# One 512-column product for h's high and low parts, and the two-step evacuation it needs

## The reference

```
h    = rms_norm(x, norm_pre_w)                     # 256 x 1024
proj = h @ w_in                                    # 1024 x 10256: q,k,v,z of mixer A; beta, decay;
                                                   # q,k,v,z of mixer B; 2 x 1024 gate logits
oa   = gated_delta_rule(silu(conv4(qkv_a)), ...)   # 8 heads of 128, chunked
ob   = moba_attention(qkv_b, T5 bias)              # 8 heads; 256 keys, so causal softmax attention
ya   = rms_norm(oa) * silu(z_a);  yb = ob * silu(z_b)
m    = sigmoid(gate_a) * (ya @ w_branch[0]) + sigmoid(gate_b) * (yb @ w_branch[1])
out  = x + rms_norm(m @ w_out, norm_post_w)
```

## Time and profile before

| | us |
|---|---|
| median of 3 runs (372.27 to 372.52) | 372.43 |
| the profiled execution, its own time | 373.05 |
| its span, from first to last instruction | 371.3 |
| PE busy (share of the span) | 360.4 (97%) |
| DVE busy | 270.6 (73%) |
| ACT busy | 220.4 (59%) |
| POOL busy | 62.3 (17%) |

### The profile page before, as it was taken

The page is one execution under the profiler, slowest core; times in us unless marked ns, Lnnn a source line. Parts: engine busy times, 40 slices in busy tenths (PEclk is TensorE's granted clock), DMA queues, the critical chain, the costliest instruction groups (busy, mean ns, idle before and its releaser), DMA issues.

```text
span 371.3 us, 7660 instructions
## 1 busy us (share of the span) xinstructions
PE 360.4 (97%) x2757; PEld 344.9 (93%) x2757; DVE 270.6 (73%) x558; ACT 220.4 (59%) x500; POOL 62.3 (17%) x121
## 2 busy tenths in 40 slices
PE   8999989999999999999999999999999999999993
PEld 5889977899999999999999999999999999999882
DVE  2868886289957778878788678797786557667644
ACT  5777695344455666767757577666676643534531
POOL 3434844520050000202020201002010100000001
PEclk9999999999999999999999999999999999999998
DMA  8658935958698445554556445564446565874633
GB/s 260 178 172 248 321 117 131 286 129 219 162 234 217 127 121 151 151 148 114 140 131 184 117 114 129 146 181 116 113 124 192 140 195 146 220 221 181 229 113 113
DMA packets 99343, 62.45 MB, mean 168 GB/s; under 512 B 3652, under 2 KB 94190, under 8 KB 99310
## 3 DMA queue, kind: packets, MB, share of 16 engines
q1 hardware_dynamic: 98014, 58.59, 57.3%
q0 software_dynamic: 1296, 3.43, 3.1%
HBM read 60.41 MB, written 1.59 MB: 167 GB/s over the span
## 4 chain that ended last, share of the span: by engine, by line
PE 85%; ACT 4%; DVE 4%; DMA 3%; issue 2%; SPq 1%; DVEq 0%; POOL 0%; ACTq 0%; POOLq 0%
PE banks L1251 61%; PE banks L1465 6%; PE banks L1268 4%; DMA raw<-in_w_in_dram 2%; ACT th_E L674 1%; DVE w_lo L861 1%; PE banks L1350 1%; PE banks L1357 1%; ACT w_hi L634 1%; DVE acc L933 1%; ACT h_hi L647 1%; PE banks L1368 1%; DMA y<-in_dn_onorm_w_dram 1%; PE banks L1393 1%; PE banks L1195 1%
## 5 line engine op out<-in xcount | busy, mean ns | idle before, releaser
L1251 PE MATMUL banks<-h_hi,w_hi 128*128 128x256 f32 x576 | 165.6, 287 | 0.3 <-PE banks L1268 0.3
L1251 PE MATMUL banks<-h_lo,w_hi 128*128 128x256 f32 x576 | 165.4, 287 | 0.0
L1251 PE MATMUL banks<-h_hi,w_lo 128*128 128x256 f32 x576 | 165.0, 287 | 0.0
L861 DVE TENSOR_TENSOR w_lo<-raw,w_hi 128x1024 fp32r<-128x1024 f32 x102 | 124.2, 1220 | 33.1 <-ACT w_hi L634 30.2
L634 ACT CAST w_hi<-raw 128x1024 fp32r<-128x1024 f32 x104 | 107.7, 1046 | 9.3 <-PE banks L1465 4.5
L1251 PEld LDWEIGHTS banks<-h_hi,w_hi 128*128 128x128 f32 x576 | 109.9, 191 | 1.5 <-issue 1.3
L1251 PEld LDWEIGHTS banks<-h_hi,w_lo 128*128 128x128 f32 x576 | 110.0, 191 | 0.0
L1251 PEld LDWEIGHTS banks<-h_lo,w_hi 128*128 128x128 f32 x576 | 109.9, 191 | 0.0
L933 DVE SCALAR_TENSOR_TENSOR acc<-banks,vec,acc 128x255 f32<-128x255 f32 (+2 forms) x72 | 34.5, 479 | 6.2 <-ACT acc L730 3.9
L1251 PE MATMUL banks<-y_hi,w_hi 128*128 128x256 f32 x128 | 36.2, 283 | 0.0
L1251 PE MATMUL banks<-y_lo,w_hi 128*128 128x256 f32 x128 | 36.2, 283 | 0.0
(11 more groups left out here) (235 smaller groups left out, 551.0 us busy)
## 6 DMA issues: line engine op xcount, KB each, us to landing
raw<-in_w_in_dram SPq DMA_DIRECT2D x80, 512.0 KB, 5.2
raw<-in_w_branch_dram SPq DMA_DIRECT2D x16, 512.0 KB, 4.9
raw<-in_w_out_dram SPq DMA_DIRECT2D x8, 512.0 KB, 3.7
xin<-in_x_dram SPq DMA_DIRECT2D x2, 512.0 KB, 3.9
xin<-bias_rows POOLq DMA_DIRECT2D x1, 1024.0 KB, 7.6
th_E<-g_rows POOLq DMA_DIRECT2D x2, 512.0 KB, 5.7
raw<-in_x_dram SPq DMA_DIRECT2D x2, 512.0 KB, 4.8
out_dram<-xin SPq DMA_DIRECT2D x4, 256.0 KB, 2.0
```

The costliest lines, as they stand in the source:

```text
L861: v.tensor_tensor(w_lo[:, t % SLOTS, cols], raw[:, t % SLOTS, cols], w_hi[:, t % SLOTS, cols].bitcast(F32), ALU.subtract).then_inc(s_lo, 1)
L1251: last = mm(ps, w, r, start=i == 0, stop=i == 23)
```

## The change

In 52 tiles (t = 2 to 5 of each head, the last 4 gate tiles, the 16 branch tiles) the two products that share the stationary block `w_hi[k]` become one of 512 columns, since the high and low parts of h (and of y) now lie side by side. The high-part sums stand in the left half of the bank, the low-part ones in the right half, and have to be added when the bank is read. A tile is 8 products of 512 columns and 8 of 256, in parts of 5, 5 and 6. ScalarE copies the right half to SBUF, VectorE adds the left half. For z the `tanh` moves one slot later and reads the sum, and the SiLU two slots later; a bank is free once the sum is made. The other 28 gate and head tiles (gates 0 to 11, t = 0 and 1 of the heads) and the 8 of k_a stay as they are.

```diff
-        h_hi = sb("h_hi", [P, KT, SEQ], F32R)
-        h_lo = sb("h_lo", [P, KT, SEQ], F32R)
+        h_parts = sb("h_parts", [P, KT, 2, SEQ], F32R)
-        y_hi = sb("y_hi", [P, 2, HEADS, SEQ], F32R)
-        y_lo = sb("y_lo", [P, 2, HEADS, SEQ], F32R)
+        y_parts = sb("y_parts", [P, 2, HEADS, 2, SEQ], F32R)
...
# ScalarE, front(h, s): tiles t = 2, 3 and t = 4, 5
-                    nc.scalar.copy(bT[:, t - 2, :], ps).then_inc(s_bT, 1)
-                else:
+                    nc.scalar.copy(bT[:, t - 2, :], bank[n % 2][:, SEQ:]).then_inc(s_b_lo, 1)
+                elif t >= 4 and s % 3 == 0:
+                    sa.wait_ge(s_tile, n + 1)
...
+                    nc.scalar.copy(gza[:, h % 2, :] if t == 4 else gzb[:], bank[n % 2][:, SEQ:]).then_inc(s_z_lo, 1)
+                elif t >= 4 and s % 3 == 1:
                     if h:
                         sa.wait_ge(s_gz, 2 * (h - 1) + t - 3)
-                    ac(tz[:, t - 4, :], ps, ACT.Tanh, scale=0.5).then_inc(s_tz, 1)
+                    sa.wait_ge(s_z_sum, 2 * h + t - 3)
+                    ac(tz[:, t - 4, :], gza[:, h % 2, :] if t == 4 else gzb[:], ACT.Tanh, scale=0.5).then_inc(s_tz, 1)
...
# ScalarE, last 4 gates: gate_front(g, 0) copies the right half, gate_front(g, 1) in the next slot,
# ahead of the w_hi there, waits for s_gate_sum and takes tanh of the sum
-                if part == 0 and n > GATES_B:
-                    gate_front(n - 1 - GATES_B + EARLY)
+                if part < 2 and n > GATES_B:
+                    gate_front(n - 1 - GATES_B + EARLY, part)
...
# ScalarE, branch loop, after split_hi
+                    sa.wait_ge(s_tile, BRANCH0 + i * 4 + t + 1)
+                    if t % 2 == 0:
+                        sa.wait_ge(s_m32, i * 2 + t // 2 + 1)
+                    nc.scalar.copy(m2[:, t % 2, :], bank[t % 2][:, SEQ:]).then_inc(s_m_part, 1)
...
# VectorE, front(h, s)
-                elif s == 9:
+                elif 2 <= t < 4 and s % 3 == 0:
+                    ve.wait_ge(s_b_lo, 2 * h + t - 1)
+                    v.tensor_tensor(bT[:, t - 2, :], ps[:, 0:SEQ], bT[:, t - 2, :], ALU.add).then_inc(s_bT, 1)
+                if s == 9:
...
                 elif t >= 4 and s % 3 == 0:
+                    ve.wait_ge(s_z_lo, 2 * h + t - 3)
+                    gz = gza[:, h % 2, :] if t == 4 else gzb[:]
+                    v.tensor_tensor(gz, ps[:, 0:SEQ], gz, ALU.add).then_inc(s_z_sum, 1)
+                elif t >= 4 and s % 3 == 2:
                     ve.wait_ge(s_tz, 2 * h + t - 3)
-                    v.scalar_tensor_tensor(out=(gza[:, h % 2, :] if t == 4 else gzb[:]), in0=tz[:, t - 4, :], scalar=1.0,
-                                           in1=ps[:, 0:SEQ], op0=ALU.add, op1=ALU.mult).then_inc(s_gz, 1)
+                    ve.wait_ge(s_z_sum, 2 * h + t - 3)
+                    gz = gza[:, h % 2, :] if t == 4 else gzb[:]
+                    v.scalar_tensor_tensor(out=gz, in0=tz[:, t - 4, :], scalar=1.0, in1=gz, op0=ALU.add,
+                                           op1=ALU.mult).then_inc(s_gz, 1)
...
# VectorE, branch loop
                     ve.wait_ge(s_tile, BRANCH0 + i * 4 + t + 1)
-                    if t % 2 == 0:
-                        ve.wait_ge(s_m_hi, d + 1)
+                    ve.wait_ge(s_m_part, i * 4 + t + 1)
+                    v.tensor_tensor(m2[:, t % 2, :], bank[t % 2][:, 0:SEQ], m2[:, t % 2, :], ALU.add).then_inc(s_m_sum, 1)
+                    ve.wait_ge(s_m_sum, i * 4 + t + 3)
...
                     v.scalar_tensor_tensor(out=one(m2[:, t % 2, :]), in0=(th_a if t % 2 else th_b)[:, bass.ds(d, 1), :],
-                                           scalar=1.0, in1=one(bank[t % 2][:, 0:SEQ]), op0=ALU.add,
+                                           scalar=1.0, in1=one(m2[:, t % 2, :]), op0=ALU.add,
                                            op1=ALU.mult).then_inc(s_m2, 1)
...
# TensorE
+            def wide_third(n, t, part, right):
...
+                for i in ((0, 1, 2, 3, 4), (5, 6, 7, 8, 9), (10, 11, 12, 13, 14, 15))[part]:
+                    k = i // 2
+                    if i % 2 == 0:
+                        mm(ps, w_hi[:, slot, P * k:P * k + P], right[:, k], start=k == 0, stop=k == KT - 1)
+                    else:
+                        last = mm(ps[:, 0:SEQ], w_lo[:, slot, P * k:P * k + P], right[:, k, 0], start=False, stop=k == KT - 1,
+                                  skip_group_check=True)
...
-                            pe.wait_ge(s_gz, 2 * (h - 1) + t + 1)
+                            pe.wait_ge(s_z_sum, 2 * (h - 1) + t + 1)
...
-                    pe.wait_ge(s_m2, i * 4 + t + 1)
+                    pe.wait_ge(s_m_sum, i * 4 + t + 1)
```

More of the change, by code:

```diff
@@ L199, in build @@
         post = vtok_all[:, 0, :]
+        h_hi, h_lo = h_parts[:, :, 0, :], h_parts[:, :, 1, :]
+        y_hi, y_lo = y_parts[:, :, :, 0, :], y_parts[:, :, :, 1, :]
         m_hi, m_lo = h_hi, h_lo
@@ L721, in front @@
                     ac(tacc[:], acc[:], ACT.Tanh, scale=0.5).then_inc(s_tanh, 1)
[L722 to L725, removed]
+                if t < 2 and s % 3 == 0:
+                    sa.wait_ge(s_tile, n + 1)
                     if t == 0:
@@ L827, in _ @@
                     gate_front(n - 1 - GATES_A)
-                if part == 0 and n > GATES_B:
-                    gate_front(n - 1 - GATES_B + EARLY)
+                if part < 2 and n > GATES_B:
+                    gate_front(n - 1 - GATES_B + EARLY, part)
                 if part == 1:
                     split_hi(n + LEAD, n + LEAD, (n + LEAD) // SLOTS + 1)
-            gate_front(2 * KT - 1)
+            for half in range(2):
+                gate_front(2 * KT - 1, half)
             sa.sem_inc(s_m_hi, 1)
@@ L1143, in _ @@
                         substitution(i)
+                if part == 0 and n > GATES_B:
+                    gate_front(n - 1 - GATES_B + EARLY)
                 if part == 2:
                     split_lo(n + LEAD, n + LEAD)
+            gate_front(2 * KT - 1)
             ve.sem_inc(s_m32, 1)
             ve.sem_inc(s_m2, 2)
+            ve.sem_inc(s_m_sum, 2)
             with ve.Fori(0, KT // 2) as i:
@@ L1253, in third, with wide @@
                     last.then_inc(s_tile, 1)
+            def wide_third(n, t, part, right):
+                ps = bank[t % 2]
+                slot = t % SLOTS
+                if part == 0:
+                    pe.wait_ge(s_hi, n + 1)
+                    pe.wait_ge(s_lo, lo_done(n))
+                for i in ((0, 1, 2, 3, 4), (5, 6, 7, 8, 9), (10, 11, 12, 13, 14, 15))[part]:
+                    k = i // 2
+                    if i % 2 == 0:
+                        mm(ps, w_hi[:, slot, P * k:P * k + P], right[:, k], start=k == 0, stop=k == KT - 1)
+                    else:
+                        last = mm(ps[:, 0:SEQ], w_lo[:, slot, P * k:P * k + P], right[:, k, 0], start=False, stop=k == KT - 1,
+                                  skip_group_check=True)
+                if part == 2:
+                    last.then_inc(s_tile, 1)
+            def wide(n):
+                return n >= GATES_B or n >= HEAD0 and (n - HEAD0) % PER_HEAD >= 2
             def value_third(n, part):
@@ L1448, in _ @@
                         bank_free(n)
-                    third(n, n, part, h_hi, h_lo, first_tile=n == 0,
-                          out_bank=K_TILES.index(n) % 2 if n < GATES_A else None)
+                    if wide(n):
+                        wide_third(n, n, part, h_parts)
+                    else:
+                        third(n, n, part, h_hi, h_lo, first_tile=n == 0,
+                              out_bank=K_TILES.index(n) % 2 if n < GATES_A else None)
             with pe.Fori(0, KT // 2) as i:
                 for t in range(4):
-                    pe.wait_ge(s_m2, i * 4 + t + 1)
+                    pe.wait_ge(s_m_sum, i * 4 + t + 1)
                     if t < 2:
-                        pe.wait_ge(s_gate_th, 2 * KT - 1 + t)
+                        pe.wait_ge(s_gate_sum, 2 * KT - EARLY - 1 + t)
                     for part in range(3):
@@ L1459, in _ @@
                             pe.wait_ge((s_ylo_b, s_ylo_a)[t], HEADS)
-                        third(BRANCH0 + i * 4 + t, t, part, y_hi[:, 1 - t % 2], y_lo[:, 1 - t % 2])
+                        wide_third(BRANCH0 + i * 4 + t, t, part, y_parts[:, 1 - t % 2])
             def out_products(k, c, e):
```

38 lines of the change are left out of this document (31 added, 7 removed).

## The result

| | us |
|---|---|
| after, median of 4 runs (378.72 to 379.43) | 378.94 |
| before, 4 runs beside it (372.19 to 372.52) | 372.35 |
| ratio, 95% interval | 1.0179 (1.0161 to 1.0196) |
| predicted, range | 372.9, 368.5 to 376.0 |

The account below looks back on a forecast made before the run. It took TensorE to bound heads and branch stage, VectorE next. Heads +0.2, gates -0.4 and branch +0.7 summed to +0.5 us, moving the median from 372.43 to 372.9 us, range 368.5 to 376.0.

Parts of the forecast that it names:

- TensorE's gain: All 52 wide tiles: products keep the two measured paces, 2.88 to 2.777 us a tile, -5.4 us in all.
- k_b and q_b: Heads, slots 9 and 12: the added evacuation work is covered, cost 0, at most 2.8 us.
- z in the heads: Heads, slots 15 to 20: work queued behind the waiting tanh stalls TensorE 3.5 us, leaving the heads at +0.2.
- Last gates: Last four gate tiles: later w_hi still leaves line 802 0.5 us ahead of its product, -0.4 us.
- Branch loop: Branch stage: VectorE becomes the bound at 6.01 us a pair of tiles, stage 46.2 against 46.1 us.
- 5.11 + 0.90: Branch loop on VectorE: 5.11 us a pair before, plus 0.90 for the adds and waits, gives 6.01.
- Output stage: Low parts of w_out queue behind the branch work; the third comes 0.6 us late for TensorE.
- 0 for the transfers: Weight loads: none added, and later release of raw slots makes no TensorE wait, cost 0.
- (a): Rival, heads and branch loop: helpers absorb the waits and the gain stays, -5.4, 367.0 us; chance 22%.
- (b): Rival, wide tiles: the mixed pace is cheaper than the sum of the two, about 369.5 us; chance 10%.
- (d): Rival, wide tiles: the fixed part per product isn't saved, a pair stays at 360 ns, 377.5 us; chance 7%.
- (c): Rival, heads: the queue behind ScalarE's waiting tanh costs 1.0 us in all eight heads, 377.4 us; chance 18%.

Follow-up runs that it names:

- e1: Kernel before with wide products in all 52 tiles but its old evacuation, low-part sums left out of the result: 369.92 us, ratio 0.9925.
- e5: Kernel before with wide tiles and their evacuation only for k_b and q_b (16 tiles): 371.86 us, ratio 0.9988.
- e10: Kernel before with wide tiles and the new evacuation only for z (16 tiles): 375.76 us, ratio 1.0093.
- e6: Changed kernel with the tanh of z and of the last gates moved behind the same slot's w_hi on ScalarE: 378.5 us, ratio 1.0164 to the kernel before.
- e11: Changed kernel with VectorE's bank credits for the branch stage given at program start: 378.14 us, ratio 1.0152 to the kernel before.
- e9: Kernel before with only branch tiles wide, bank credits at program start, and each tile's two weight splits one tile earlier: 371.49 us, ratio 0.9978.
- e8: Kernel before with only branch tiles wide, early bank credits, and the branch sum and its low part moved from VectorE to GpSimd: 377.74 us, ratio 1.0147.
- e4: Kernel before with wide tiles only in the branch stage, heads and gates as before: 375.10 us, ratio 1.0066.

## Why the prediction was wrong

By the marks of the result, the prediction's own terms against what was measured, in us:

| stretch | predicted | measured |
|---|---|---|
| head 0 to head 7 (28 of the heads' 32 tiles, stalls 3.5) | +0.6 | +2.9 |
| from there to the first branch product (4 tiles and the gates) | -0.8 | +0.9 |
| branch stage (46.2 against 46.1) | +0.1 | +2.0 |
| output stage | +0.6 | +1.0 |

- **TensorE's gain** (0.104 us a tile, -5.4). The first step that failed: "I take the sum of the two measured paces". Products of two widths in turn cost 352.5 ns a pair. That is 5.4 ns above the sum, so 8 pairs gain 0.06 us a tile and 52 tiles 3.1; e1 measured 2.4 to 2.8. In the prediction's sum the branch tiles' gain was already gone, so only the 36 tiles of heads and gates carry this error: 1.6 us by the pace, about 2 by what e1 gained a tile. By the Trainium skill's 2.5 ns per product (TensorE: Matmul & The Clock Gate, "Wait — 56ns, not 53.3ns?"), dropping 8 products would be worth 20 ns a tile, an estimate. The trace shows 60, so its direction was a warning worth more than I gave it, though its size is wrong here: the pair stands (352.5 - 320)/2 = 16 ns a product above bare columns.
- **k_b and q_b** (cost 0): near. e5 gains 0.5 us where the pace alone would give 0.96, and what e1 gained a tile 0.7; the difference of 0.2 to 0.5 wasn't traced.
- **z in the heads** (stalls 3.5). Mechanism confirmed: e10 puts the whole loss on z, and TensorE stops where forecast, for 1.42 us in head 0 (forecast 1.1), 0.66 in head 2 (0.6), 0.58 in head 3 (0.65) and 0.57 in head 4 (0.7); head 1 has no stop (0.15), and head 5 one of 0.55, of which 0.40 was there before (0.3). Size: near. TensorE idles 3.5 us more than before, and a stop costs some 0.15 more than its idle time (the one at 300.81 shows 0.92 and puts the product 1.07 late), so with five stops more the loss is about 4.3; against e1 the interval is 4.1 longer. So of the 2.3 us by which the interval missed, the smaller gain of the 28 tiles is 1.2 (by the pace) to 1.7 (by e1), the larger part, and the stalls 0.6 to 0.8. The second wait that e6 showed, VectorE's last product ahead of `w_lo`, was made by the move: in the kernel after all waits of that product come to 2.7 us, before to 1.9.
- **Last gates** (-0.4): wrong sign. The step that failed is that the gates' new steps were followed to one consumer only, "line 802 still 0.5 us ahead of its product". The bank credit behind the last gate's add isn't in the prediction: it makes TensorE stop for 0.92 us, and the first branch product is 1.07 us late. e11, with the credit early, takes this stretch back to 22.2 us.
- **Branch loop** (6.01 us a pair, stage 46.2). Right that the helpers' loop and not TensorE paces the stage. The failed step is the sum "5.11 + 0.90", which takes VectorE's time as its own work. Its 5.11 held waits for ScalarE (0.42 and 0.62 in the earlier trace rows); in the pair of 6.15 they are 1.1 us. e9 runs the same work of VectorE at TensorE's pace, so the ring through ScalarE, and not VectorE's load, sets the loop. That 6.01 came near 6.23 is in part luck. The size that was off: an add and its dependent product are 0.54 and 0.58 us apart and not 0.45 each, 0.22 us a pair, which is the whole difference of the two numbers, some 1.5 us in seven pairs. The stage is 48.1, +2.0 and not +0.1.
- **Output stage** (+0.6): +1.0. The forecast's stop is there: the third tile's first product starts 0.63 us late (forecast 0.6), for a `w_hi` that stood behind the last `m_hi`. The other 0.4 us are small differences at both ends. ScalarE's `w_hi` waits 2.6 us in three for `w_out`'s transfer, whose slot is freed by a late `w_lo`; in the kernel before it waits for none. But no wait of TensorE follows from it, so the prediction's 0 for the transfers holds.

The rivals: (a) and (b) are refuted by the waits and the pace, (d) by the 0.06 us a tile that stayed, though its 377.5 is the nearest number. (c), 377.4, named the right side, a product in the heads that meets a helper's slipped queue; but its price of 1.0 us in all eight heads didn't occur (some 4.2 us in seven), and more than half of the loss lies in the branch stage and its two ends. The range ended too low because the errors all had one sign: a pace that was too good, a credit that was left out, and a loop step that was too short. That they had a common cause isn't shown.

## What to carry to other kernels

An evacuation split over two in-order engines adds a crossing to every later step. Price each crossing on both sides: what is queued behind the wait on each engine, and what that queue also feeds (weight splits, credits). Here, moving the wait within one engine moved it to the other (e6). A credit that depends on nothing belongs at the start of the program, not behind a wait (e11). In a loop over several engines, add up the ring, not the busiest engine's work: moving 0.8 us of work a pair off VectorE cost 2.6 us (e8 against e4), doing the splits one tile earlier gave 3.6 (e9). And a pace from runs of like products isn't the pace of their mixture; keep like ones together.

## What the runs showed of the hardware

- Wide and narrow products in turn: 352.5 ns a pair; sorted by width, 230 and 119 ns.
- The Trainium skill gives about 131 ns for a sustained product of 512 columns with its weight load (TensorE: Matmul & The Clock Gate, "Back-to-back issue gap"). The traces don't agree: at a granted clock of 1.00 they show 227 and 230 ns, and these hold for this case.
- The same 128x256 add out of and into SBUF takes 0.42 us on VectorE and 0.74 us on GpSimd.
- On VectorE, a product that waits for the semaphore of the add just before it starts 0.54 to 0.58 us after it; the add of the two branches, which waits in the same way for the product before it, 0.46 us (DVE of the kernel after, above).
